# A two-block transformer in one kernel: latent attention's scores as three products of rounded parts, blocks' output factors by turns, the last tile's end by halves

## The reference

```python
def _adaln(cond, w_mod, b_mod):                 # gives shift, scale, gate
    m = jax.nn.silu(cond) @ w_mod + b_mod
    return jnp.split(m, 3, axis=-1)
def _post_norm(x, y, gate, g, b):
    return _layer_norm(ALPHA * x + gate * y, g, b)
def one(qi):                                    # latent attention, 128 queries at a time, 8 heads
    s = jnp.einsum('bqhd,bkhd->bhqk', qi, k, preferred_element_type=jnp.float32) * scale
    p = jax.nn.softmax(s, axis=-1).astype(v.dtype)
    return jnp.einsum('bhqk,bkhd->bqhd', p, v)  # k has 256 context + 512 latent rows, d = 64 + 32 (rope)
...
f = swiglu(rmsnorm(x, ffn2_pre_g[l]), ffn2_w_gate[l], ffn2_w_up[l], ffn2_w_down[l])
x = x + FFN_RESIDUAL_WEIGHT * rmsnorm(f, ffn2_post_g[l])      # the last of these is the output
```

## Time and profile before

| | |
|---|---|
| median of three runs | 2511.12 us |
| the profiled execution's own time | 2510.31 us |
| its span, first to last record | 2508.4 us |
| TensorE busy | 2481.6 us, 99% |
| VectorE busy | 1611.6 us, 64% |
| ScalarE busy | 1164.0 us, 46% |
| GpSimd busy | 116.8 us, 5% |
| granted TensorE clock over the run | 0.999 |

### The profile page before, as it was taken

One profiled execution on the slowest core, in us unless ns is written; L12 is line 12 of the kernel. 1 busy time (PEld: TensorE's weight loads), 2 busy tenths in 40 slices (PEclk: granted clock), 3 DMA queues, 4 the chain that ended last, 5 costly groups with the idle time before them and its releaser, 6 DMA issues.

```text
span 2508.4 us, 41613 instructions
## 1 busy us (share of the span) xinstructions
PE 2481.6 (99%) x17116; PEld 2179.5 (87%) x17116; DVE 1611.6 (64%) x2799; ACT 1164.0 (46%) x1991; POOL 116.8 (5%) x176
## 2 busy tenths in 40 slices
PE   9999999999999999999999999999999999999998
PEld 7788887678999888887999988999888887899987
DVE  3425664668899344577799735899544477698833
ACT  4223334642555334576455533555333477455522
POOL 0140000001000000001000000000000001000000
PEclk9999999999999999999999999999999999999999
DMA  8721141111333323222333332333333221333321
GB/s 333 298 97 57 61 126 42 35 60 60 109 102 103 117 84 107 68 68 68 101 102 110 110 106 79 118 102 102 112 107 93 66 67 61 100 102 105 115 101 67
DMA packets 182155, 252.30 MB, mean 101 GB/s; under 512 B 13008, under 2 KB 156624, under 8 KB 177488
## 3 DMA queue, kind: packets, MB, share of 16 engines
q1 hardware_dynamic: 181968, 249.65, 30.2%
HBM read 247.53 MB, written 2.10 MB: 100 GB/s over the span
## 4 chain that ended last, share of the span: by engine, by line
PE 92%; DVE 3%; ACT 1%; DMA 1%; issue 1%; POOL 1%; SPq 0%; POOLq 0%; DVEq 0%; ACTq 0%
PE psum L831 88%; DMA mod_w<-in_l_ab_w_mod 1%; PE psum L1418 1%; PE psum L1301 1%; PE psum L899 1%; ACT w_hi L1595 1%; PE psum L1520 0%; DVE stats_first L2239 0%; DVE work L2232 0%; POOL stats_first L2997 0%; DMA u_gated<-in_l_cd_w_mod 0%; DVE X L2235 0%; DVE w_lo L2138 0%; ACT work L1643 0%; PE psum L875 0%
## 5 line engine op out<-in xcount | busy, mean ns | idle before, releaser
L831 PE MATMUL psum<-h_hi,w_hi 128*128 128x256 f32 (+1 forms) x1520 | 496.7, 327 | 1.2 <-DVE w_lo L2138 1.2
L831 PE MATMUL psum<-h_hi,w_lo 128*128 128x256 f32 (+1 forms) x1520 | 490.2, 322 | 0.0
L831 PE MATMUL psum<-h_lo,w_hi 128*128 128x256 f32 (+1 forms) x1520 | 490.2, 322 | 0.0
L2138 DVE TENSOR_TENSOR w_lo<-raw,w_hi 128x2048 fp32r<-128x2048 f32 (+2 forms) x99 | 223.3, 2259 | 310.9 <-ACT w_hi L1595 310.3
L831 PEld LDWEIGHTS psum<-h_hi,w_hi 128*128 128x128 f32 x1520 | 289.4, 190 | 28.3 <-issue 5.5
L831 PEld LDWEIGHTS psum<-h_hi,w_lo 128*128 128x128 f32 x1520 | 289.3, 190 | 22.8
L1595 ACT ACTIVATE w_hi<-raw 128x2048 fp32r<-128x2048 f32 (+2 forms) x100 | 188.2, 1887 | 258.7 <-PE psum L831 248.4
L831 PEld LDWEIGHTS psum<-h_lo,w_hi 128*128 128x128 f32 x1520 | 289.6, 191 | 20.2 <-issue 0.5
L831 PE MATMUL psum<-w_hi,ff_hi 128*128 128x512 f32 x576 | 224.9, 390 | 1.3 <-DVE ff_lo L2778 1.3
L831 PE MATMUL psum<-w_lo,ff_hi 128*128 128x512 f32 x576 | 224.1, 389 | 0.0
L831 PE MATMUL psum<-w_hi,ff_lo 128*128 128x512 f32 x576 | 224.1, 389 | 0.0
(11 more groups left out here) (366 smaller groups left out, 5056.1 us busy)
## 6 DMA issues: line engine op xcount, KB each, us to landing
raw<-in_ffn_w_gate SPq DMA_DIRECT2D x44, 1024.0 KB, 5.3
raw<-in_ffn_w_up SPq DMA_DIRECT2D x44, 1024.0 KB, 5.4
raw<-in_ffn_w_down SPq DMA_DIRECT2D x44, 1024.0 KB, 4.9
raw<-in_w_in SPq DMA_DIRECT2D x36, 512.0 KB, 5.1
raw<-in_l_ab_w_in SPq DMA_DIRECT2D x10, 1024.0 KB, 8.9
mod_w<-in_l_ab_w_mod SPq DMA_DIRECT2D x8, 1024.0 KB, 17.7
raw<-in_w_out SPq DMA_DIRECT2D x8, 1024.0 KB, 4.8
u_gated<-in_l_cd_w_mod SPq DMA_DIRECT2D x6, 1024.0 KB, 5.9
```

The lines of the kernel that those rows point to most:

```text
L831: return pe.matmul(o, lhsT, rhs, start=start, stop=stop, skip_group_check=True)
L2138: dve.tensor_tensor(lo[:, 0:nk * n], raw[c % 2][:, 0:nk * n], hi[:, 0:nk * n].bitcast(F32), ALU.subtract).then_inc(*w_lo_made.mark(key))
```

## The change

Three edits, in separate stages.

1. **Scores in three products.** `kT` and `qT` become fp32r: what ScalarE and VectorE copy there is rounded. The rests go to `k_low` and `q_low`. They lie in rooms that are free at this time: new tiles `low_parts` and `low_query`, and the upper halves of `main_lo` and `main_hi` (h_lo and h_hi in the rows). VectorE makes them by subtraction: for keys and queries from PSUM, behind ScalarE's copy; for rope rows from SBUF. A bank with keys or queries is now freed by VectorE's subtraction. GpSimd sets zero rows. TensorE makes each score product by `mm3`.
2. **Output factors by turns.** `gate_row` transposes 4 columns of factors, each read as a 128 by 128 block with the same column throughout. `gate_diags` is gone, and with it two kinds of `work` tile.
3. **The last tile by halves.** Of the last FFN's last tile the first half's columns are finished with all four chunks before the second half's. Squares, the product with the gain, the last add and the store go by halves of 512 columns; the inverse root comes behind both squares, with one more GpSimd addition ahead of it.

```diff
@@ def gate_row
-                pe.wait_ge(*diag_made[event])
-                done(mm(bank(b), ones[:, :], work_tile(event)[:, :], True, True), event)
+                pe.wait_ge(*mod_made[11 if mod is mod_ab else 23])
+                for j in range(4):
+                    k = 16 + 4 * h + j
+                    m = pe.transpose(bank(b, P, j * P), mod[:, k, s:s + 1].broadcast_to([P, P]), ident[:, :])
+                done(m, event)
@@ down, TensorE
+                    if s == LAST and i == NT - 1:
+                        for h in range(2):
+                            for c in last:
+                                m = down_part(s, nk, hi, lo, c, i, i * P, ready, False, (h,))
+                            done(m, ("y", s, i, "half") if h == 0 else ("y", s, i))
+                        continue
@@ latent attention, TensorE, step n
+                        pe.wait_ge(*k_low_made[hd, 1])
+                        pe.wait_ge(*q_low_made["rope", hd])
+                        pe.wait_ge(*q_low_made["head", hd])
...
-                        m = mm(bank(b + r, width), qT[hd % 4][0:depth, t * P:(t + 1) * P], kT[hd % 4][0:depth, off:off + width], True, True)
+                        m = mm3(bank(b + r, width), qT[i][0:depth, at], q_low[i][0:depth, at], kT[i][0:depth, off:off + width],
+                                k_low[i][0:depth, off:off + width], True, True)
@@ VectorE
+            def pair_key_lows(p):
+                for r, (off, n) in enumerate(RANGES):
+                    event = ("keys", p, r)
+                    dve.wait_ge(*k_made[2 * p + 1, r])
+                    for hd in (2 * p, 2 * p + 1):
+                        p0 = 64 * (hd % 2)
+                        dve.tensor_tensor(k_low[hd % 4][p0:p0 + NOPE, off:off + n], rows(event, p0, p0 + NOPE, n),
+                                          kT[hd % 4][p0:p0 + NOPE, off:off + n].bitcast(F32), ALU.subtract).then_inc(*k_low_made.mark((hd, r)))
+                    freed[event] = k_low_made[hd, r]
+            def pair_query_lows(p):
+                event = ("queries", p)
+                dve.wait_ge(*q_made["head", 2 * p + 1])
+                for hd in (2 * p, 2 * p + 1):
...
+                freed[event] = q_low_made["head", hd]
@@ VectorE, ahead of the Fourier gates: both key_rope_low, pair_rope_lows(0), pair_key_lows(0), pair_query_lows(0)
@@ VectorE, end of step n
-                if n < len(seq) - 8 and n % 8 == 5:
-                    pair_ropes(n // 8 + 1)
+                if n < len(seq) - 8:
+                    if n % 8 == 2:
+                        pair_key_lows(n // 8 + 1)
+                    if n % 8 == 4:
+                        pair_query_lows(n // 8 + 1)
+                    if n % 8 == 5:
+                        pair_ropes(n // 8 + 1)
+                    if n % 8 == 6:
+                        pair_rope_lows(n // 8 + 1)
+                if n in (3, 5):
+                    key_rope_low(2 + n // 5)
@@ the last tile: ScalarE, VectorE, GpSimd, SyncE
+                    act.activation(wide[1][:, h * BANK:(h + 1) * BANK], bank(2 * t + h), ACT.Square, scale=2 * D ** -0.5,
+                                   accum_out=stats[:, 24 + h:25 + h]).then_inc(*squared.mark(event))
+                    dve.tensor_tensor(wide[0][:, sl], bank(2 * t + h), post_g[:, sl], ALU.mult).then_inc(*residual.mark(("gained", LAST, t, h)))
+                    dve.scalar_tensor_tensor(out=X[:, t, sl], in0=wide[0][:, sl], scalar=stat("rms", t, 2, 3), in1=X[:, t, sl], op0=ALU.mult,
+                                             op1=ALU.add).then_inc(*residual.mark(("x", LAST, t, h)))
+                pool.tensor_tensor(stat("rms", t, 1, 2), stat("rms", t, 0, 1), stats[:, 25:26], ALU.add).then_inc(*pool_biased.mark(("y", LAST, t)))
+                sp.dma_start(out[0, (NT - 1) * P:, h * BANK:(h + 1) * BANK], X[:, NT - 1, h * BANK:(h + 1) * BANK]).then_inc(*stored.mark("all"))
```

More of the change, by code:

```diff
@@ L366, in build @@
         keys_scope = ExitStack()
-        kT = [sb(keys_scope, "kT", [P, LA]) for _ in range(4)]
+        kT = [sb(keys_scope, "kT", [P, LA], F32R) for _ in range(4)]
         q_rope = sb(keys_scope, "q_rope", [P, 2, L])
@@ L432, in build @@
         mla = ExitStack()
-        qT = [sb(mla, "qT", [P, L]) for _ in range(4)]
+        qT = [sb(mla, "qT", [P, L], F32R) for _ in range(4)]
         v_all = sb(mla, "v_all", [P, 6, HEADS * 64])
@@ L437, in build @@
         mla.close()
+        hi_room, lo_room = [t[:, 4:8, :].rearrange("p a b -> p (a b)") for t in (main_hi, main_lo)]
+        k_low = [f_low[:, 0:LA], f_low[:, LA:2 * LA], lo_room[:, 0:LA], lo_room[:, LA:2 * LA]]
+        q_low = [f_low[:, 2 * LA:], c_low[:, :], lo_room[:, 2 * LA:], hi_room[:, 2 * LA:]]
         cd.close()
@@ L611, in build @@
         work_order += [("latents", t) for t in range(6)]
-        work_order += [("gate_cd", 0), ("gate_cd", 1), ("rope", "kr"), ("rope", 0), ("rope", 1)] + [("fnet", g) for g in range(4)]
+        work_order += [("rope", "kr"), ("rope", 0), ("rope", 1)] + [("fnet", g) for g in range(4)]
         work_order += [("attn", t) for t in range(NT)] + [("lnw", "cd", t, h) for t in range(NT) for h in range(2)]
@@ L1048, in tensor_program @@
                 elif kind == "gate":
-                    gate_row(("gate", step[1], step[2]))
+                    gate_row(step, mod_ab, step[2], step[1])
                 elif kind == "end":
@@ L1682, in turn_hi, with last_squares @@
                                    ACT.Copy).then_inc(*h_hi_made.mark(event))
+            def last_squares(t):
+                act.wait_ge(*residual["x", LAST, t - 1])
+                for h in range(2):
+                    event = ("y", LAST, t, "half") if h == 0 else ("y", LAST, t)
+                    act.wait_ge(*psum_full[event])
+                    act.activation(wide[1][:, h * BANK:(h + 1) * BANK], bank(2 * t + h), ACT.Square, scale=2 * D ** -0.5,
+                                   accum_out=stats[:, 24 + h:25 + h]).then_inc(*squared.mark(event))
             def residual_square(s, t):
                 event = ("y", s, t)
+                if s == LAST and t == NT - 1:
+                    last_squares(t)
+                    return
                 if t:
@@ L2379, in vector_program @@
                     last_mod[0] = step[1]
-                elif kind == "gate":
-                    _, s, h = step
-                    if s == h == 0:
-                        dve.wait_ge(*mod_made[11])
-                    gate_diags(step, mod_ab, h, s)
                 elif kind == "group":
@@ L3045, in gpsimd_program @@
                 pool.wait_ge(*slots_zeroed[("query", i - 1) if i > 1 else ("key", 3)])
-                pool.memset(qT[i][32 * ZERO_AT[i]:32 * ZERO_AT[i] + 32, :], 0.0).then_inc(*slots_zeroed.mark(("query", i)))
+                pool.memset(qT[i][32 * ZERO_AT[i]:32 * ZERO_AT[i] + 32, :].bitcast(F32), 0.0).then_inc(*slots_zeroed.mark(("query", i)))
             pool.wait_ge(*slots_zeroed["query", 3])
+            for i in range(1, 4):
+                at = slice(32 * ZERO_AT[i], 32 * ZERO_AT[i] + 32)
+                if i == 1:
+                    pool.wait_ge(*rope_step["rope", 1])
+                else:
+                    pool.wait_ge(*psum_full["fnet", 3])
+                    pool.wait_ge(*lows_zeroed[i - 1])
+                pool.memset(k_low[i][at, :].bitcast(F32), 0.0).then_inc(*lows_zeroed.mark(("key", i)))
+                pool.wait_ge(*lows_zeroed["key", i])
+                pool.memset(q_low[i][at, :].bitcast(F32), 0.0).then_inc(*lows_zeroed.mark(i))
             def mean_rsqrt(event, kind, t, weight=1.0):
```

75 lines of the change are left out of this document (59 added, 16 removed).

## The result

| | before | after |
|---|---|---|
| median, lowest to highest, runs | 2511.10 us, 2510.44 to 2511.52, 14 | 2516.31 us, 2513.55 to 2520.12, 14 |
| ratio to before, 95% interval | | 1.0023, 1.0016 to 1.0030 |
| the profiled execution, its span | 2510.31, 2508.4 us | 2520.12, 2517.1 us |
| first maximum of attention | 440.18 us | 436.48 us |
| first turns of attention to the last item's | 100.35 us | 114.51 us |

The changed kernel is slower by 5.2 us, a little over 0.2%. I had forecast no change, 2511.0 us; 2516.31 lies near the upper end of my range of 2503 to 2517.5.

What follows compares the result with a forecast made beforehand. TensorE, busy for 2481.6 of 2508.4 us, was taken as the bound. Terms: -7.8 (scores) + 12.9 (waits) - 3.2 (factors) - 2.0 (end) = -0.1 us, so a median of 2511.0 us, no change; range 2503 to 2517.5.

Steps and rivals of the forecast that it cites:

- free step: An attention step without waits: period of 2.74 us, set by TensorE, in place of 2.99.
- saving on the scores: Attention's score products on TensorE: fp32r in place of fp32 saves 0.25 us a step, 31 x 0.25 = 7.8 us.
- keys' stops: Scores of items 3, 11, 19: TensorE waits for VectorE's key rests to free banks, 1.7, 2.35, 2.35, together 6.4 us.
- queries' stops: Inside the scores of items 5, 13, 21: TensorE waits for VectorE's query rests, three waits of 1.0, 3.0 us.
- backlog: Attention: VectorE's added operations make maxima late, so TensorE's transposes wait for exponentials, 3.5 us in sum.
- slower rival: Subtractions from PSUM with fp32r output cost 1.11 us, not 0.68: 6.2 us more, 2517.2; chance 16% for the slower case.
- The clock: Rival in attention: each of three long TensorE stops costs one step at half speed, 2.74 each, 2519.2 us; chance 4%.
- Cast: VectorE's copy of rope rows becomes a cast: 0.86 us for two, as the copy; otherwise 1.0 us more in all.
- factors: Output factors by turns on TensorE: 2.5 us from cheaper operations and a 0.76 wait gone, sum 3.2 us saved.
- end: Behind the last product: work by halves gains 1.5 us for the last add, 2.0 us together with the store.

Runs made afterwards that it cites:

- junk kernel: The changed kernel plus unread products of ones by ones in TensorE's stops ahead of the scores of items 3, 11 and 19: 2513.73 us, ratio 1.0011.
- `e_staged`: The changed kernel, but for pairs 1 to 3 ScalarE's plain copies free the banks and VectorE makes key and query rests from them: 2504.86 us, ratio 0.9976.
- `e_rope_pool`: The changed kernel with the rope rows' rests (queries' pairs 1 to 3, keys 2 and 3) on GpSimd, not VectorE: 2514.85 us, ratio 1.0017.
- `e_all_pool`: The changed kernel with plain copies by ScalarE freeing the banks and all rests of pairs 1 to 3 on GpSimd: 2500.43 us, ratio 0.9958 to before.

## Why the prediction was wrong, step by step

The stage, step by step, from the distances between the turns of one item and the next. A free step is the standard; what lies above it is a wait with what hangs on it. The junk kernel has the waits at full clock. I had written that I would be wrong if the stage got over 9 us longer: it did, by 9.8 and 14.2 us, while at full clock it is 8.2.

| us | forecast | junk kernel | changed, slowest | changed, fastest |
|---|---|---|---|---|
| free step | 2.74 | 2.75 | 2.75 | 2.75 |
| saving on the scores | -7.8 | -7.1 | -7.1 | -7.1 |
| keys' stops, steps 1, 9, 17 | 1.7 + 2.35 + 2.35 = 6.4 | 2.05 + 2.74 + 2.74 = 7.5 | 7.5 | 7.5 |
| queries' stops, steps 3, 11, 19 | 3.0 | 3.45 | 3.45 | 3.45 |
| backlog, steps 5, 6, 14, 21, 22 | 3.5 | 0.75 + 1.18 + 0.88 + 0.48 + 1.06 = 4.35 | 4.35 | 4.35 |
| half clock behind the stops | 0 | 0 | 5.9 | 1.6 |
| stage against before | +5.1 | +8.2 | +14.2 | +9.8 |

- *Saving on the scores: right in kind, too large by 0.5.* A step is 0.235 us shorter and not 0.25. Of the 31 products that I counted, 30 lie in the stage; item 0's lies ahead of the first turns, so another 0.25 of the table's 0.7 is only in another place. The change between fp32 and fp32r within a step cost nothing to be seen.
- *The keys' stops: right places, right cause, too short by 1.1.* In the long ones I had TensorE served 4.05 us behind the start of the turns. In the chain above the turns begin at 473.60 (the maximum's 473.80 less 0.20) and the scores at 477.94: 4.34. The rests, after:

```profile
475.58 2.30 DVE L2645 TENSOR_TENSOR low_parts<-psum,kT 64x512 fp32r<-64x512 f32 x4
```

  The first starts where I had it, at 1.98 (forecast 1.99). The four start at 475.58, 476.29, 477.01 and 477.46, that is 0.71, 0.72 and 0.45 apart rather than 0.60, 0.60 and 0.34. They end at 4.30 in place of 3.95; the way to TensorE took 0.04 and not 0.10. The last 0.10 of the 0.39 is that TensorE would have come at 1.60 (an undisturbed step's scores start at 458.20, its turns at 456.60) and not at 1.70. The pace I had from operations at other places. The dear rest of my slower rival (1.11) didn't come: 0.67 to 0.70.
- *The queries' stops:* 1.0 forecast, 0.9 of waiting, but the step is 1.15 longer. The trace of step 3 has the other 0.25. The wait is counted from the end of the third product (454.86 + 0.39), while in an undisturbed step the next one starts 0.23 behind its start: 0.16. And the first product behind the wait holds up the second for 0.22 (456.14 to 456.36) in place of 0.12.
- *The backlog: the waits were right,* 0.60, 0.96, 0.72, 0.33 and 0.85 in the junk kernel, 3.46 in sum as forecast. But six turns behind a wait take 0.84 and not 0.66, and this is 0.18 on each of five. The row that shows it stood in my list, and I had used it for the time of the transposes' start alone.
- *The clock: the step that failed.* I had it as a rival with 4%, on the ground that the clock averaged 0.999 over the run before "with all its stops in it". TensorE's dearest waits in the run before; the third line is attention's:

```profile
PE psum L899 <- DVE wide L2269: 3.6, 4, 1.7
PE psum L831 <- DMA ident<-in_k_ident: 3.4, 1, 3.4
PE psum L1301 <- ACT probs L1890: 2.0, 2, 1.1
```

  The longest between products is 1.7 us, and in attention 1.1; the 3.4 are the wait for the first transfer, with no product ahead of it. In windows of 50 us the clock was 1.00 from 0 to 2500 us. Such a run, and an average over it, says nothing of three stops of 1.8 to 2.7 us within 66 us: the step went from the kinds of stops that were there to one that was not, and put this term at nothing. The runs show 2.2 to 2.7 us of the median for it. The price I gave it, one step at half speed for each stop, +8.2, was too high for the median: of the eight falls in four profiles seven cost 1.5 to 1.6 us and one 2.8 (the third of the slowest execution), and not every stop has its fall. The rule that I cited from the Trainium skill, "TensorE: Matmul & The Clock Gate", section "A second HAM failure mode: psum-queue depth-cycling", tells of frequent short waits. The changed kernel's trace agrees in that the clock goes down and up behind waits at the banks, 0.50 behind each of three stops, but here these are rare and long: `e_staged`, with 12 waits of up to 1.4 us, kept 1.00.
- *Cast, factors and end: right.* The two casts take 0.87 us, the price of the copies, as the rule of the Trainium skill cited there ("VectorE: DVE Perf Modes", section "The perf-mode tier table (the rule you actually need)") had it. Factors -3.0 against -3.2, end -2.0 against -2.0.

In the sum: forecast -0.1. The stage at full clock is 3.1 us dearer than counted: 2.4 by the stops and the turns behind waits, 0.7 by the smaller saving. Of the 2.4, 1.1 are the keys' stops, 0.45 the queries' and 0.85 the backlog's, nearly all of it the turns behind waits. The half clock adds 2.2 us to the median by the junk kernel's time (5.2 less 3.0), 2.7 by the steps (the first turns 3.7 earlier, the stage 8.2 longer and the end 2.0 shorter make +2.5 at full clock; the median has +5.2). Together 5.3 to 5.8; that the first turns came 0.5 earlier than the forecast has the factors bring them goes off. Item 0's 0.25 is in this 0.5, and the first turns came another 0.5 apart in the two profiles of the changed kernel. The median is 5.3 over the forecast. So two steps failed: the clock's term was put at nothing, and the stage at full clock was mis-sized by 3.1. The clock and the 0.85 of the backlog have one root, that a stop of TensorE was priced at its own length; the rests' pace and the smaller saving are errors of size.

Open is what decides whether the clock falls behind a given stop. Of the twelve keys' stops in the two profiles of the changed kernel, the one of the scores alone and the one of `e_rope_pool`, eight had a fall behind them and four had none, with waits of the same lengths; the third stop had it each time.

## What to carry to other kernels

Where one bank feeds both a rounded copy and a rest, let a plain copy by an engine with room give the bank back, and make the rest from it later, on the engine that is idle; the same arithmetic then gave -10.5 us where the rest read from PSUM gave +5.2. Price a new stop of TensorE by more than its length: the turns behind it start slower (0.18 us here), and the clock may fall behind it, as it did behind eight of twelve stops of 1.8 to 2.7 us here, so that the time also scatters. An average clock says nothing of a kind of stop that the run doesn't contain.

## What the runs showed of the hardware that I had not expected

- The granted clock fell to 0.50 behind stops of 1.8 to 2.7 us in a stage where TensorE's other waits were of 1.4 us at most, in some executions and not in others, for 3 to 7 us each time. With junk products in the stops it stayed at 1.00, and the executions' spread went from 6.6 to 1.3 us.
- VectorE's subtraction of 128 by 512 in SBUF took 0.87 to 1.66 us beside GpSimd's subtractions in `e_all_pool`, and 0.68 to 0.69 without them.
- GpSimd subtracts 64 by 512 values in 1.27 to 1.61 us, with fp32r output (`e_all_pool`), where VectorE takes 0.67 to 0.70, reading one input from PSUM (the changed kernel).
